# The partition exchange of the rope by four transfers on ScalarE's queue

## The reference

```python
def _rot_half(x, cos, sin):
    x1, x2 = jnp.split(x, 2, axis=-1)
    return jnp.concatenate([x1 * cos - x2 * sin, x2 * cos + x1 * sin], axis=-1)

def apply_axial_rope(x, tables):
    cr, sr, cc, sc = [t[None, :, None, None, :].astype(x.dtype) for t in tables]
    xr, xcol = jnp.split(x, 2, axis=-1)
    return jnp.concatenate([_rot_half(xr, cr, sr), _rot_half(xcol, cc, sc)], axis=-1)
```

## Time and profile before

| | |
|---|---|
| Median of 3 runs | 2555.73 us (2554.55 to 2558.8) |
| Profiled execution | 2553.34 us, span 2551.7 us |
| TensorE busy | 2502.2 us, 98% |
| VectorE busy | 2056.2 us, 81% |
| ScalarE busy | 1263.9 us, 50% |
| Stretch of K slabs' ropes | 264 to 436 us |
| Stretch of Q slabs' ropes | 436 to 583 us |

### The profile page before, as it was taken

One profiled execution on the slowest core, in us unless ns is written; L12 is line 12 of the kernel. 1 busy time (PEld: TensorE's weight loads), 2 busy tenths in 40 slices (PEclk: granted clock), 3 DMA queues, 4 the chain that ended last, 5 costly groups with the idle time before them and its releaser, 6 DMA issues.

```text
span 2551.7 us, 38428 instructions
## 1 busy us (share of the span) xinstructions
PE 2502.2 (98%) x13946; PEld 2159.0 (85%) x13946; DVE 2056.2 (81%) x2708; ACT 1263.9 (50%) x1705; POOL 198.6 (8%) x302
## 2 busy tenths in 40 slices
PE   6999999998999999999999999999999999999998
PEld 4778888777898888888888988888988888888886
DVE  6888887887898889987888799989988877674554
ACT  5422334676565555554444544445655555554443
POOL 1002221000000001110111011101000000000000
PEclk9999999999999999999999999999999999999999
DMA  9768987554778878887999699968688856655554
GB/s 353 272 221 264 302 268 234 157 157 140 240 247 266 268 250 273 288 263 221 297 291 298 228 310 345 335 219 285 223 278 265 265 180 191 188 189 201 196 191 147
DMA packets 442816, 625.65 MB, mean 245 GB/s; under 512 B 18692, under 2 KB 359062, under 8 KB 435504
## 3 DMA queue, kind: packets, MB, share of 16 engines
q1 hardware_dynamic: 401888, 450.94, 53.3%
q0 software_dynamic: 40464, 172.59, 21.0%
q10 hardware_dynamic: 320, 0.13, 0.0%
HBM read 621.50 MB, written 2.10 MB: 244 GB/s over the span
## 4 chain that ended last, share of the span: by engine, by line
PE 89%; DVE 5%; ACT 3%; DMA 2%; issue 2%; SPq 0%; ACTq 0%; DVEq 0%; POOLq 0%
PE ps L1988 46%; PE ps L1996 24%; PE ps L2332 6%; PE ps L2339 3%; PE ps L1908 2%; PE ps L1910 1%; PE ps L1909 1%; DVE w_lo L1153 1%; ACT w_hi L642 1%; PE ps L2064 1%; PE ps L2063 1%; PE ps L2065 1%; DVE ada_sum L1224 1%; PE ps L1834 1%; DMA first_x<-in_w_ada_dram 1%
## 5 line engine op out<-in xcount | busy, mean ns | idle before, releaser
L642 ACT ACTIVATE w_hi<-raw 128x1024 fp32r<-128x1024 f32 (+1 forms) x792 | 821.9, 1048 | 917.3 <-PE ps L1996 412.2
L1153 DVE TENSOR_TENSOR w_lo<-raw,w_hi 128x1024 fp32r<-128x1024 f32 (+1 forms) x792 | 955.5, 1212 | 385.3 <-ACT w_hi L642 382.4
L1988 PE MATMUL ps<-xs,w_hi 128*128 128x512 f32 x3200 | 764.2, 393 | 1.3 <-DVE v_rows L1201 1.3
L1988 PEld LDWEIGHTS ps<-xs,w_hi 128*128 128x128 f32 x3200 | 592.8, 188 | 126.2 <-issue 7.0
L1996 PEld LDWEIGHTS ps<-xs,w_lo 128*128 128x128 f32 x3200 | 403.4, 191 | 11.8 <-issue 1.0
L1996 PE MATMUL ps<-xs,w_lo 128*128 128x256 f32 x3200 | 409.7, 283 | 0.0
L2332 PE MATMUL ps<-w_hi,act 128*128 128x512 f32 x704 | 175.2, 390 | 0.0
L1988 PE MATMUL ps<-xs_sin,w_hi 128*128 128x512 f32 x704 | 169.7, 392 | 0.5 <-DVE xs_sin L1402 0.5
L1988 PE MATMUL ps<-act,w_hi 128*128 128x512 f32 x704 | 165.1, 390 | 0.0
L2332 PEld LDWEIGHTS ps<-w_hi,act 128*128 128x128 f32 x704 | 131.6, 188 | 27.1
L540 POOL DMA_DIRECT2D ada_ring<-in_w_ada_dram x128 | 91.0, 711 | 791.6 <-DVE ada_sum L1224 538.6
(11 more groups left out here) (266 smaller groups left out, 2981.1 us busy)
## 6 DMA issues: line engine op xcount, KB each, us to landing
raw<-in_ffn_w_up_dram SPq DMA_DIRECT2D x352, 512.0 KB, 4.7
ada_ring<-in_w_ada_dram POOLq DMA_DIRECT2D x176, 512.0 KB, 5.4
raw<-in_ffn_w_down_dram SPq DMA_DIRECT2D x152, 512.0 KB, 3.7
raw<-in_attn_w_qkv_dram SPq DMA_DIRECT2D x96, 512.0 KB, 4.9
broad_ring<-in_w_ada_dram POOLq DMA_DIRECT2D x48, 1024.0 KB, 6.1
raw<-in_sconv_w_in_dram SPq DMA_DIRECT2D x96, 512.0 KB, 5.6
ada_ring_kv<-in_w_ada_dram POOLq DMA_DIRECT2D x48, 512.0 KB, 5.4
raw<-in_attn_w_o_dram SPq DMA_DIRECT2D x32, 512.0 KB, 4.4
```

The lines of the kernel that those rows point to most:

```text
L642: nc.scalar.activation(w_hi[:, slot, 0:n_tiles, :], raw[:, slot, 0:n_tiles, :], ACT.Copy).then_inc(hi_made, 1)
L1153: nc.vector.tensor_tensor(w_lo[:, slot, 0:n_tiles, :], raw[:, slot, 0:n_tiles, :], w_hi[:, slot, 0:n_tiles, :], ALU.subtract).then_inc(lo_ ...
L1988: last = mm(ps[:, bank + m, :], w_hi[:, slot, t, P * m:P * m + P], src[:, tile + t, :], start=(is_first and t == 0), stop=(is_last and t = ...
```

## The change

`rotate` issues four transfers on ScalarE's queue, one for each block of 32 partitions (2 KB per partition, 64 KB each), from `y_qk` to `rot`. Each adds 16 to `rot_made` on landing, so VectorE waits for 64 more per slab.

```diff
                 se.wait_ge(acc_read, n + 1)
                 for d in range(4):
-                    last = nc.scalar.activation(rot[32 * d:32 * d + 32, :, :], y_qk[32 * (d ^ 1):32 * (d ^ 1) + 32, :, :], ACT.Copy)
-                last.then_inc(rot_made, 1)
+                    se.dma_start(rot[32 * d:32 * d + 32, :, :], y_qk[32 * (d ^ 1):32 * (d ^ 1) + 32, :, :]).then_inc(rot_made, 16)
...
                 if between is not None:
                     between()
-                ve.wait_ge(rot_made, r + 1)
+                ve.wait_ge(rot_made, 64 * r + 64)
                 nc.vector.tensor_tensor(rot[:, :, :], rot[:, :, :], two(rope_sin), ALU.mult).then_inc(rope_part, 1)
```

## The result

The changed kernel takes 2583.03 us (median of 5 runs, 2582.32 to 2588.72) against 2555.73 (median of 5, 2551.40 to 2558.80): 27.3 us or 1.1% slower, ratio 1.0112, 95% interval 1.0098 to 1.0127. The forecast was 2559 with a range of 2552 to 2569.

The account below looks back on a forecast made before the run. TensorE, busy 98%, was taken as the bound, so only its waits count. Terms 0 + 0.8 + 0 + 1.85 + 0.5 = 3.2 us gave 2556.5 for the profiled execution; with 2.39 to the median, 2559 us, range 2552 to 2569.

Parts of the forecast that it names:

- The issue: On ScalarE's queue: each of four transfer issues takes 0.42 us, 1.7 us per slab, from rows of 0.37 and 0.49.
- L: Time from the end of VectorE's add_b until the rotated block is complete: 2.6 us before, forecast 4.2, ends 3.2 and 6.1.
- the row nearest in size and kind is rope_cos, 128 KB in 2.9 us with the queues loaded, and I take 2.9: Landing time of the fourth transfer after its issue: 2.9 us, between bounds of 2.1 and 4.6.
- last slab: Q slab at 578 us: probabilities late again, TensorE 0.5 us late on top of the rounds before.
- K costs nothing up to L = 5.9: Eight K slabs: VectorE's other work to 4.67 us, then 1.23 us idle time, cover the rotation; cost 0.
- Q's working: Sum over the Q slabs of TensorE's lateness from late sine products: 0.8 + 0 + 1.85 + 0.5 us.
- x less slack: Second Q slab: sine product 1.58 us late, less 0.77 us before TensorE's transposes, makes TensorE 0.8 us late.
- first slabs: Q slabs before the four rounds: 0.8 us in one, 0 in the next.
- four rounds: Q slabs at 497, 517, 538, 558, paced by VectorE and ScalarE in turn: 0.35 + 3 x 0.5 = 1.85 us.
- Rival A: Transfers queue like loads, landing after 4.6 us: 15 us slower, 2571; chance 0.37 including what lies between.
- ScalarE's relief: ScalarE, four issues replacing four copies of 2.56 us: free 0.85 us earlier per slab (0.6 to 1.1).
- Rival B: ScalarE's relief decides, at L = 3.2: 2.5 us faster, 2553; chance 0.13.

Follow-up runs that it names:

- two half changes: Changed kernel with the four transfers in one stage only, ScalarE's copies in the other: transfers in K 2563.55 us (ratio 1.0031), transfers in Q 2574.52 us (1.0083).
- late rope: Changed kernel with VectorE's sine product and add moved behind other ready work in K and Q: 2561.90 us, ratio 1.0026.
- late order in the first slab: Changed kernel with the rope's end moved behind the four multiply-adds in the first K slab only: 2580.03 us, ratio 1.0100.

## Why the prediction was wrong

- **What bounds the kernel: right.** TensorE's waits carried the loss, and the path through VectorE's order decided. That the stages add up is shown by the two half changes.
- **The issue: mis-sized.** Taken 0.42 us, measured 0.61. Three of them are 1.84 us of L in place of 1.26. The row of 0.49 was taken as the upper end and was none: it was one of four issues at the kernel's start.
- **The step that failed is "the row nearest in size and kind is rope_cos, 128 KB in 2.9 us with the queues loaded, and I take 2.9", with one L for both stages.** Landings are 5 to 7 us in K and 3.2 to 5 in Q, apart from the 2.0 to 3.9 at the change-over and the last slab's 5 to 6. So L was 8.3 to 9.1 in K and 5.1 to 7.8 in Q, not 4.2. The two runs with light loads and the one with tiny transfers show why: 2.0 us is the transfer, the rest is the other queues' loads. K's DMA share of 83% stood in the earlier trace rows, and the upper bound of 4.6 us was read in Q (54%) and used for K. The loads that VectorE releases just ahead of a rotation were named, and priced at 0.8 us (2.9 less 2.1). The DMA view of before also has a nearer row, of the same size and on ScalarE's own queue, at the start of the kernel:

```profile
ident<-in_ident_dram ACTq DMA_DIRECT2D x1, 64.0 KB, 4.1
```

  With it L = 5.4, and the prediction's sum would have given about 11 us, an estimate. The busy share alone is no price either: with the late rope K's landings are 2.9 us at a share of 85%.
- **"K costs nothing up to L = 5.9": right that there is such a cover, too small by 0.5 to 0.9 us.** By its own rule the seven slabs, 2.4 to 3.2 us past 5.9 each, would have cost 19.6 us; K paid 9 to 11. The sum left out that VectorE of the kernel before also stands for 0.49 us right behind the split, ahead of the sum into k_t, and that in every second round the first wait is 1.6 us:

```profile
361.02 1.23 DVE L1153 TENSOR_TENSOR w_lo<-raw,w_hi 128x1024 fp32r<-128x1024 f32 x1 [1.63 <-ACT w_hi L642]
362.74 0.69 DVE L1329 TENSOR_TENSOR k_t<-k_t,ps 128x512 f32 x1 [0.49 <-ACT k_t L703]
```

  The changed kernel has neither wait in the slabs that were late. With both, the cover reaches to L = 6.4 and 6.8 by turns, an estimate; in the run with the late order in the first slab, a slab with L = 6.4 cost TensorE nothing. The seventh slab has 7.4 us of idle time behind it and cost nothing either. The forecast of 0 for K failed all the same, by L. The range had no case in which K's cover goes, since no L above 6.1 was in it.
- **An estimate that left out feedback.** L was a constant in the sum. In the kernel VectorE's lateness moves its loads towards the rotation, as the places of the loads with early and late rope show, and the waits grew from 1.05 to 4.42 us. That this is most of K's 5.5 us is argued, not shown: the run that took away only the first wait delayed the growth by two slabs and did not stop it.
- **Q's working: right with the measured L.** The second slab's 2.52 us is x less slack, 2.54. With each slab's measured L in the prediction's terms, the sum is 2.5 + 2.7 for the first slabs, 7.3 for the four rounds and 4.7 for the last slab, 17 us, an estimate; Q alone cost 20.2. The first Q slab, set to 0, is most of the rest: L = 6.6 made TensorE wait 2.0 us for q_head. Rival A, L = 5.9 in all slabs, named 15 us. With L = 3.9 the sum gives about 1 us, and the run with little traffic measured 1.3, with an interval from -0.5 to 4.3.
- **ScalarE's relief: right that it is small, too large all the same.** Its wait for the issues is 2.44 us against 2.56 for the copies, so 0.1 us a slab was freed and not 0.85. Rival B needed that relief and a landing near 2 us, and had neither. TensorE's waits for a_t went from 4.5 to 3.2 us.
- **Open:** 8 of the 35 us between the two profiled spans are not in the medians; 4 of them come after 650 us, where TensorE waited 3.1 us for w_hi at 1629 and 1691 us, in the gated convolution. What made these two waits was not looked into.

## What to carry to other kernels

A small transfer between tiles costs its issues one after another plus a landing that is set by what the other queues have in flight at that moment, here 2.0 us with the loads cut, and 5 to 7 or 2.9 us in the same stage at nearly the same busy share, by what VectorE's order had released before it. Read the price in the same stage, and look at which loads the program releases just ahead of the transfer. Before replacing copies on an engine that is half idle, look at what stands behind them in its order: moving one ready copy ahead of the wait won 2.4 us (0.5 to 5.1 by the interval), where taking all the copies away lost 27. A wait in an in-order engine costs by what it stands in front of; with other ready work put ahead of it, three quarters of the loss went.

## What the runs showed of the hardware that was not expected

- Four issues in a row on ScalarE's queue take 0.51 us for the first and 0.61 for the others (up to 1.4 in some runs), a single 128-partition one 0.47. Over 32 partitions 64 KB and 2 KB give the same 0.61. As time on the engine, four are worth four copies of 32 x 512 elements, 0.63 us each.
- Landing of a 64 KB transfer within SBUF: 2.0 us at the median with the loads cut (DMA share 0.20 to 0.24); with them 4.9 to 7.2 in K (0.82) and 3.2 to 5.0 in Q (0.53), and 2.9 at the median in K with the late rope (0.85). Of 2 KB with them: 3.9 to 5.6 in K.
- TensorE's clock over the 10 us that hold a wait of 6.7 us had a mean of 0.68, and the matmuls behind the wait took up to 1.7 times as long: that stall cost more than its own time. A wait of 2.7 us in the first K slab came with 0.86 over 11 us in the kernel before, one of 2.6 us with 1.00 in the run with a_t copied first: 24.46 against 22.86 us for the same work.
